# MLP down projection: a third seven-product pair in each quad job, and product banks released by two sums

## The chip, the core and the metric

One core of one Trainium2 chip. The metric is device time in microseconds for one execution of the program. The engines in play: TensorE (PE, matmuls and weight loads), VectorE (DVE), ScalarE (ACT), GpSimd (POOL, a few small operations) and SyncE (SP), which issues the loads of the weights.

## The reference, cut to what matters

Two transformer-like blocks on 256 tokens of width 2048, in float32. The change lies in the MLP of the first one:

```python
u = jax.nn.relu(rms_norm(h, mlp_norm_g) @ w_up)    # 256 x 8192
h = h + (u * u) @ w_down                           # 8192 x 2048
```

Behind it follow an HGRN2 mixer and a convolutional FFN, which the change does not touch.

## The kernel before

Every weight is streamed once, in **windows** of 128 x 1024 float32 (512 KB). SP loads a window into one of six `raw` slots. ACT copies it, rounded, to `w_high` (line 1275), DVE takes `raw - w_high` to `w_low` (line 1594); both have five slots (`AHEAD`), so the split of window s waits until PE is done with window s-5. A product is then three matmuls: high x high, high x low, low x high. Activations are split the same way (`act_high`, `act_low`).

A program (`PLAN`) lists jobs, each a run of windows that adds up in PSUM banks, and puts the other steps at windows. `walk` gives every engine the same order: at window w first the steps put early, then the splits of w+5, then the steps put late. An engine works through its list in order, so a step put between two splits delays all that follow.

The MLP has four blocks of 2048 hidden columns (`FF_BLOCKS`). For each block, four pairs of "features" jobs make the up projection (u, squared, split: `u_square`, `u_split`). The down projection of a block comes next. In blocks 1 to 3 it is two **quad jobs** (c = 0 and c = 2), each for 2 x 512 output columns; block 4 has one quad job and two ordinary token jobs.

A quad job multiplies u (2 tiles of 128 tokens x 16 row chunks) with 16 x 2 blocks of w_down of 128 x 512. Its 16 row chunks are taken in eight pairs (`QUAD_ORDER`). An "eight" pair makes its eight block products in two windows of four products each. A "seven" pair makes the 2x2 by 2x2 block product with seven (Strassen-Winograd forms): two loaded windows and two windows that DVE makes in `raw` from those (`sums_of`, four sums), of which the last is half used. Its windows hold 2, 2, 2 and 1 products. On the activation side it needs sums of blocks of u, the forms (`u_forms`, once a block, for both seven pairs).

Banks: the ordinary sums C of a quad job fill four banks (its own `J` pair, and two of `att`). The products P1, P5, P6 and P7 of the seven pairs gather in the other four, which the job before or behind uses as its C. So PE must wait, at the first window of a job's first seven pair, until the finished banks of the job before have been added to H (`OTHER_EMPTIED`, `add_quads`, line 1930), and at the next job's start until the P banks are read (`add_sevens`). `add_sevens` comes behind the last seven window: ACT copies P1 (line 1482), DVE makes the sums with P6, P7 and P5 and adds them to H (lines 1913 to 1920), eight operations. `h_added` at their end releases the banks.

A job before is 20 windows: eight, seven, eight, eight, seven, eight, eight, eight.

Of the kernel before, what the change touches and what calls it, by code (L numbers as in the profile page):

```python
# [61 lines left out]
QUAD_ORDER = (("eight", 2), ("seven", 0), ("eight", 3), ("eight", 4), ("seven", 1), ("eight", 5), ("eight", 6), ("eight", 7))  # L62
SEVENS = [p for what, p in QUAD_ORDER if what == "seven"]

# [64 lines left out]
class Plan:  # L129
# [71 lines left out]
    "add_sevens": dict(p_copied=1, h_added=1),  # L201
# [142 lines left out]
def plan_mlp(p):  # L344
    for b in range(FF_BLOCKS):
        for j in range(4):
# [4 lines left out]
            p.put(job.end + 1 + 2 * behind, "u_split", j)  # L351
            if j == 0:
                p.put(job.end + 2, "u_forms", b)
# [236 lines left out]
def added():  # L590

    counts, at = Counts(), {}

    def stage(w, name, *args):
        if name in ("add_sevens", "add_quads"):
            at[WINDOW[w][0], name] = counts.at("h_added", 1)
    walk(counts, lambda w: None, lambda w, s: None, stage)
    return at
# [8 lines left out]
def build(nc, d, out):  # L607
    ctx = ExitStack()
    with ctx:
# [12 lines left out]
        forms_both = sb("forms_both", [P, 2, 1024], F32R)  # L622
        H = sb("H", [P, TT, D])
# [70 lines left out]
        form_at = lambda f, p: slice(((f - 1) * 2 + SEVENS.index(p)) * P, ((f - 1) * 2 + SEVENS.index(p) + 1) * P)  # L694
        p1, u_one, u_two = slots[:, 4, 0:COLS], slots[:, 4, COLS:2 * COLS], slots[:, 5, 0:COLS]
# [162 lines left out]
        def _(pe):  # L858
# [30 lines left out]
            def first_of(w):  # L889
# [3 lines left out]
                if k == 0 and job in BEHIND_QUADS:  # L893
                    once("h_added", ADDED[BEHIND_QUADS[job], "add_sevens"])
                if job.kind == "quads" and k == 0 and job in PREVIOUS_QUADS:
                    once("h_added", ADDED[PREVIOUS_QUADS[job], "add_sevens"])
# [48 lines left out]
            def quads(w):  # L945
# [3 lines left out]
                for x, (bank, (of, i, where), cc) in enumerate(job.products(k)):  # L949
# [4 lines left out]
                    else:  # L954
                        once("forms_low", job.needs[1] + 1)
                        ah, al = (a[:, form_at(i, where)] for a in (forms_high, forms_low))
# [290 lines left out]
        def _(act):  # L1247
# [32 lines left out]
            def stage(w, name, *a):  # L1280
# [193 lines left out]
                elif name == "u_forms":  # L1474
                    wait(act, n, "forms_made")
                    wait(act, n, "h_added", 0)
                    nc.scalar.activation(forms_high, forms, ACT.Copy).then_inc(S["forms_high"], 1)
                elif name == "add_sevens":
# [3 lines left out]
                    nc.scalar.activation(p1, quad_bank(buf, ("P", 1)), ACT.Copy).then_inc(S["p_copied"], 1)  # L1482
# [88 lines left out]
        def _(dve):  # L1571
# [59 lines left out]
            def stage(w, name, *a):  # L1631
# [255 lines left out]
                elif name == "u_forms":  # L1887
# [3 lines left out]
                    u = a_slot(2).rearrange("p (q c x t) -> p q c x t", q=2, c=2, x=TT)  # L1891
                    a11, a12, a21, a22 = (u[:, :, c, x, :] for x, c in ((0, 0), (0, 1), (1, 0), (1, 1)))
                    s1, s2, s3, s4 = (forms[:, i * T:(i + 1) * T].rearrange("p (q t) -> p q t", q=2) for i in range(4))
# [6 lines left out]
                    nc.vector.tensor_tensor(forms_low, forms, forms_high.bitcast(F32), ALU.subtract)\  # L1900
# [270 lines left out]
```

## Time and profile before

| | |
|---|---|
| median of 3 runs | 2496.78 us (2496.45 to 2496.8) |
| the profiled execution | 2497.42 us, its span 2495.6 us |
| PE busy | 2476.8 us, 99% of the span |
| DVE busy | 1752.0 us, 70% |
| ACT busy | 1258.2 us, 50% |
| granted TensorE clock, mean | 0.997 |
| weights loaded | 855 windows of 512 KB, median 4.2 us from issue to landing |

Busy time is the time in which an engine has an instruction under way; a matmul's end is modelled, so a busy PE may still be short of its peak, and starts are the safer measure. A row of the timeline gives start and duration, and in brackets the idle time of the engine ahead of it and what ended that. Consecutive instructions of the same kind are merged into one row with their count. The quad jobs lie at 549 to 633, 722 to 807, 896 to 980 and 1069 to 1111 us.

### The profile page before, as it was taken

To read this page: it belongs to the slowest core of one execution; us is meant where nothing else is said; L and a number is where in the kernel's file an instruction comes from. 1 tells how busy PE (TensorE), PEld (TensorE's weight loads), DVE (VectorE), ACT (ScalarE), POOL (GpSimd) and SP (SyncE) were. 2 spreads that over 40 slices of the span, in tenths; PEclk is the share of its full clock that TensorE was granted. 3 is DMA by queue.
4 is the path that set the end of the run, shared out by engine and by line. 5 is a ranking of instruction groups with operands and counts; after the bars stand their busy time and mean duration, and the time that the engine had idled before them with its cause. 6 is when DMAs were issued, how large, how long until landed. Compare 5 with 4: busy or idle time off the path is not lost.

```text
span 2495.6 us, 38061 instructions
## 1 busy us (share of the span) xinstructions
PE 2476.8 (99%) x15416; PEld 2116.1 (85%) x15416; DVE 1752.0 (70%) x1978; ACT 1258.2 (50%) x1506; POOL 29.5 (1%) x26
## 2 busy tenths in 40 slices
PE   9999999999999999999999999999999999999998
PEld 7888888888888888888888888887888888888886
DVE  6656765668668577675777777775777666777777
ACT  7654344545444444445454545454654444444553
POOL 0000000000000000000000000000000000000000
PEclk9999999999999999999999999999999999999999
DMA  9454545546646546565545454555465555556553
GB/s 382 155 189 152 170 157 190 177 162 226 196 169 226 193 171 217 178 211 169 187 154 185 154 185 154 185 185 194 145 216 189 187 193 191 184 190 201 185 188 127
DMA packets 128240, 465.98 MB, mean 187 GB/s; under 512 B 14369, under 2 KB 14625, under 8 KB 127169
## 3 DMA queue, kind: packets, MB, share of 16 engines
q1 hardware_dynamic: 127920, 463.53, 55.1%
q8 instruction: 122, 2.00, 0.3%
q14 instruction: 54, 0.43, 0.1%
q10 hardware_dynamic: 144, 0.02, 0.0%
HBM read 461.39 MB, written 2.10 MB: 186 GB/s over the span
## 4 chain that ended last, share of the span: by engine, by line
PE 96%; issue 3%; DVE 1%; DMA 0%; ACT 0%; SPq 0%; DVEq 0%; POOL 0%; POOLq 0%
PE job L971 31%; PE job L983 16%; PE job L939 11%; PE job L940 11%; PE job L941 11%; PE job L958 2%; PE job L959 2%; PE job L960 2%; PE att L958 2%; PE att L960 2%; PE att L959 2%; PE att L1178 1%; PE att L999 0%; PE att L1011 0%; PE att L1120 0%
## 5 line engine op out<-in xcount | busy, mean ns | idle before, releaser
L1275 ACT ACTIVATE w_high<-raw 128x1024 fp32r<-128x1024 f32 (+1 forms) x883 | 919.8, 1050 | 728.4 <-PE job L941 288.5
L1594 DVE TENSOR_TENSOR w_low<-raw,w_high 128x1024 fp32r<-128x1024 f32 (+1 forms) x883 | 1045.4, 1213 | 303.9 <-ACT w_high L1275 225.9
L971 PE MATMUL job<-actA,w_high 128*128 128x512 f32 x3328 | 799.3, 392 | 0.0
L971 PEld LDWEIGHTS job<-actA,w_high 128*128 128x128 f32 x3328 | 612.8, 189 | 119.5
L983 PEld LDWEIGHTS job<-actA,w_low 128*128 128x128 f32 x3328 | 426.7, 191 | 16.2
L983 PE MATMUL job<-actA,w_low 128*128 128x256 f32 x3328 | 431.7, 283 | 0.0
L1797 DVE TENSOR_TENSOR slots<-job,slots 128x512 f32<-128x512 f32 x102 | 70.5, 691 | 344.0 <-ACT slots L1467 343.3
L939 PE MATMUL job<-w_high,actB 128*128 128x512 f32 x736 | 287.9, 391 | 2.2 <-DVE w_low L1594 1.6
L940 PE MATMUL job<-w_low,actB 128*128 128x512 f32 x736 | 286.5, 389 | 0.0
L941 PE MATMUL job<-w_high,actB 128*128 128x512 f32 x736 | 286.4, 389 | 0.0
L939 PE MATMUL job<-w_high,actA 128*128 128x512 f32 x576 | 230.9, 401 | 0.0
L941 PE MATMUL job<-w_high,actA 128*128 128x512 f32 x576 | 224.5, 390 | 0.0
L940 PE MATMUL job<-w_low,actA 128*128 128x512 f32 x576 | 224.4, 390 | 0.0
L1467 ACT ACTIVATE slots<-job 128x512 f32<-128x512 f32 x102 | 61.0, 598 | 240.6 <-PE job L983 240.6
L939 PEld LDWEIGHTS job<-w_high,actB 128*128 128x128 f32 x736 | 138.2, 188 | 31.8 <-DVE w_low L1594 2.0
L941 PEld LDWEIGHTS job<-w_high,actB 128*128 128x128 f32 x736 | 138.2, 188 | 28.8
L940 PEld LDWEIGHTS job<-w_low,actB 128*128 128x128 f32 x736 | 138.2, 188 | 27.9
L941 PEld LDWEIGHTS job<-w_high,actA 128*128 128x128 f32 x576 | 108.1, 188 | 23.3
L939 PEld LDWEIGHTS job<-w_high,actA 128*128 128x128 f32 x576 | 108.1, 188 | 22.5
L940 PEld LDWEIGHTS job<-w_low,actA 128*128 128x128 f32 x576 | 108.2, 188 | 20.7
L958 PE MATMUL job<-w_high,actB 128*128 128x512 f32 x210 | 81.7, 389 | 0.0
L959 PE MATMUL job<-w_low,actB 128*128 128x512 f32 x210 | 81.7, 389 | 0.0
(257 smaller groups left out, 1906.1 us busy)
## 6 DMA issues: line engine op xcount, KB each, us to landing
raw<-in_weights SPq DMA_DIRECT2D x855, 512.0 KB, 4.2
M<-in_mem_t SPq DMA_DIRECT2D x8, 256.0 KB, 7.9
slots<-in_mem SPq DMA_DIRECT2D x2, 1024.0 KB, 12.2
M<-in_x_t SPq DMA_DIRECT2D x4, 512.0 KB, 13.6
H<-in_x SPq DMA_DIRECT2D x2, 1024.0 KB, 9.0
out<-H SPq DMA_DIRECT2D x8, 256.0 KB, 3.2
slots<-in_w_small SPq DMA_DIRECT2D x1, 1024.0 KB, 10.3
slots<-in_post_mix_g SPq DMA_DIRECT2D x1, 1024.0 KB, 4.8
```

The source lines that it names most:

```text
L939: nc.tensor.matmul(to, ah, w_high[:, slot, cols], start=begins and cc == 0, stop=False)
L940: nc.tensor.matmul(to, ah, w_low[:, slot, cols], start=False, stop=False)
L941: mm = nc.tensor.matmul(to, al, w_high[:, slot, cols], start=False, stop=ends and cc == job.per - 1)
L958: nc.tensor.matmul(to, ah, w_high[:, w % AHEAD, cols], start=(k, x) in job.firsts, stop=False)
L959: nc.tensor.matmul(to, ah, w_low[:, w % AHEAD, cols], start=False, stop=False)
L960: mm = nc.tensor.matmul(to, al, w_high[:, w % AHEAD, cols], start=False, stop=(k, x) in job.lasts)
L971: mm = nc.tensor.matmul(J[job.buf][:, x, :], w_high[:, w % AHEAD, cols], act_both[job.act][:, c, :, :].rearrange("p a t -> p (a t)"), star ...
L983: mm = nc.tensor.matmul(J[job.buf][:, x, T:2 * T], w_low[:, w % AHEAD, cols], act_high[job.act][:, c, :], start=False, stop=ends and cc == ...
L1275: nc.scalar.activation(w_high[:, s % AHEAD, cols], raw[:, s % RAW_SLOTS, cols], ACT.Copy)\
L1467: nc.scalar.activation(by_feature(JOIN[to][:, half_ * COLS:(half_ + 1) * COLS]), J[buf][:, :, T:2 * T], ACT.Copy).then_inc(S["low_copied"], 1)
L1594: nc.vector.tensor_tensor(w_low[:, s % AHEAD, cols], raw[:, s % RAW_SLOTS, cols], w_high[:, s % AHEAD, cols].bitcast(F32), ALU.subtract).t ...
L1797: nc.vector.tensor_tensor(x, J[buf][:, :, 0:T], x, ALU.add).then_inc(S["joined"], 1)
```

## The change

Three pairs of eight are done by seven products, where two were, and they alternate with eights: eight 3, seven 0, eight 4, seven 1, eight 5, seven 2, eight 6, eight 7. A quad job gets 22 windows with 61 products (before 20 with 62). The second seven starts at window 8 (before 10), the third at 14, and four windows (before six) follow the last seven. There are seven quad jobs.

The third pair's forms have a place of their own (`more_forms`, `more_high`, `more_low`) and are made after the second quarter of u (`u_forms` with j = 1). The last quarter's split is moved by two windows. ACT copies P5 too, and the next job waits for the new event `sevens_read`, counted when DVE has made its two sums with P6 and P7, where it waited for `h_added` at the end of all eight operations.

```diff
--- before.py
+++ after.py
@@ -59,9 +59,7 @@
 
 MEM_SET, X_SET, MLP_SET, PREMIX_SET, PREFFN_SET = range(5)
 
-QUAD_ORDER = (("eight", 2), ("seven", 0), ("eight", 3), ("eight", 4), ("seven", 1), ("eight", 5), ("eight", 6), ("eight", 7))
-SEVENS = [p for what, p in QUAD_ORDER if what == "seven"]
-
+QUAD_ORDER = (("eight", 3), ("seven", 0), ("eight", 4), ("seven", 1), ("eight", 5), ("seven", 2), ("eight", 6), ("eight", 7))
 O_EVENT = {2: 1, 3: 2, 0: 3, 1: 4}
 
 
@@ -198,7 +196,7 @@
     "u_square": dict(u_squared=1),
     "u_split": dict(u_high=1, u_low=1),
     "u_forms": dict(forms_made=1, forms_high=1, forms_low=1),
-    "add_sevens": dict(p_copied=1, h_added=1),
+    "add_sevens": dict(p_copied=1, sevens_read=1, h_added=1),
     "add_quads": dict(h_added=1),
     "f_sigmoid": dict(f_sigmoid=1),
     "f_make": dict(f_ready=1),
@@ -348,9 +346,9 @@
                               f"u{j % 2}", False)
             behind = 3 if j == 3 else 0
             p.put(job.end + behind, "u_square", j)
-            p.put(job.end + 1 + 2 * behind, "u_split", j)
-            if j == 0:
-                p.put(job.end + 2, "u_forms", b)
+            p.put(job.end + 1 + 3 * behind - behind // 3, "u_split", j)
+            if j < 2:
+                p.put(job.end + 2, "u_forms", b, j)
         paired = (0, 2) if b < FF_BLOCKS - 1 else (0,)
         for c in paired:
             job = p.quads("B", "w_down", c * COLS, range(b * KC, (b + 1) * KC), ("u_low", b), b * KC)
@@ -593,7 +591,7 @@
 
     def stage(w, name, *args):
         if name in ("add_sevens", "add_quads"):
-            at[WINDOW[w][0], name] = counts.at("h_added", 1)
+            at[WINDOW[w][0], name] = counts.at("sevens_read" if name == "add_sevens" else "h_added", 1)
     walk(counts, lambda w: None, lambda w, s: None, stage)
     return at
 
@@ -620,6 +618,7 @@
         act_both = {n: sb(f"act{n}", [P, KC, 2, T], F32R) for n in "AB"}
         act_high, act_low = ({n: act_both[n][:, :, part, :] for n in "AB"} for part in (0, 1))
         forms_both = sb("forms_both", [P, 2, 1024], F32R)
+        more_both = sb("more_both", [P, 2, COLS], F32R)
         H = sb("H", [P, TT, D])
         M = sb("M", [P, TT, D])
         slots = sb("slots", [P, 10, 1024])
@@ -691,8 +690,16 @@
         post_g = a2(6)
 
         forms, forms_high, forms_low = m_slot(0), forms_both[:, 0, :], forms_both[:, 1, :]
-        form_at = lambda f, p: slice(((f - 1) * 2 + SEVENS.index(p)) * P, ((f - 1) * 2 + SEVENS.index(p) + 1) * P)
-        p1, u_one, u_two = slots[:, 4, 0:COLS], slots[:, 4, COLS:2 * COLS], slots[:, 5, 0:COLS]
+        more_forms = m_slot(1)[:, 0:COLS]
+        more_high, more_low = more_both[:, 0, :], more_both[:, 1, :]
+
+        def form_of(part, f, p):
+
+            if p < 2:
+                at = ((f - 1) * 2 + p) * P
+                return (forms_high, forms_low)[part][:, at:at + P]
+            return (more_high, more_low)[part][:, (f - 1) * P:f * P]
+        p1, u_one, u_two, p5 = (slots[:, 4 + i // 2, i % 2 * COLS:(i % 2 + 1) * COLS] for i in range(4))
         z_conv, y_gate, y_value, y_sig, y = a_slot(0), a_slot(1), a_slot(2), a_slot(3), a_slot(4)
 
         JOIN = {"u0": a_slot(0), "u1": a_slot(1), "f0": hg["f"][0], "f1": hg["f"][1], "q": hg["q"], "z": z_conv,
@@ -891,9 +898,9 @@
                 if k == 0 and job in EMPTIED:
                     once(*EMPTIED[job])
                 if k == 0 and job in BEHIND_QUADS:
-                    once("h_added", ADDED[BEHIND_QUADS[job], "add_sevens"])
+                    once("sevens_read", ADDED[BEHIND_QUADS[job], "add_sevens"])
                 if job.kind == "quads" and k == 0 and job in PREVIOUS_QUADS:
-                    once("h_added", ADDED[PREVIOUS_QUADS[job], "add_sevens"])
+                    once("sevens_read", ADDED[PREVIOUS_QUADS[job], "add_sevens"])
                 if job.kind == "quads" and part_of(w) == 0:
                     once(*OTHER_EMPTIED[job])
                     if job in PREVIOUS_QUADS:
@@ -952,8 +959,8 @@
                         once("u_low", 4 * job.needs[1] + i // 4 + 1)
                         ah, al = (a["B"][:, i, where * P:(where + 1) * P] for a in (act_high, act_low))
                     else:
-                        once("forms_low", job.needs[1] + 1)
-                        ah, al = (a[:, form_at(i, where)] for a in (forms_high, forms_low))
+                        once("forms_low", 2 * job.needs[1] + 1 + where // 2)
+                        ah, al = (form_of(part, i, where) for part in (0, 1))
                     to = quad_bank(job.buf, bank)
                     nc.tensor.matmul(to, ah, w_high[:, w % AHEAD, cols], start=(k, x) in job.firsts, stop=False)
                     nc.tensor.matmul(to, ah, w_low[:, w % AHEAD, cols], start=False, stop=False)
@@ -1474,12 +1481,14 @@
                 elif name == "u_forms":
                     wait(act, n, "forms_made")
                     wait(act, n, "h_added", 0)
-                    nc.scalar.activation(forms_high, forms, ACT.Copy).then_inc(S["forms_high"], 1)
+                    to, of = ((forms_high, forms), (more_high, more_forms))[a[1]]
+                    nc.scalar.activation(to, of, ACT.Copy).then_inc(S["forms_high"], 1)
                 elif name == "add_sevens":
                     buf, c = a
                     act.wait_ge(window_done, w + 1)
                     wait(act, n, "h_added", 0)
-                    nc.scalar.activation(p1, quad_bank(buf, ("P", 1)), ACT.Copy).then_inc(S["p_copied"], 1)
+                    nc.scalar.activation(p1, quad_bank(buf, ("P", 1)), ACT.Copy)
+                    nc.scalar.activation(p5, quad_bank(buf, ("P", 5)), ACT.Copy).then_inc(S["p_copied"], 1)
                 elif name == "f_sigmoid":
                     direction = a[0]
                     f, k = hg["f"][direction], hg["KS"][direction]
@@ -1888,16 +1897,19 @@
 
                     wait(dve, n, "u_squared", 0)
                     wait(dve, n, "forms_high", 0)
-                    u = a_slot(2).rearrange("p (q c x t) -> p q c x t", q=2, c=2, x=TT)
+                    raw_forms, high, low = ((forms, forms_high, forms_low), (more_forms, more_high, more_low))[a[1]]
+                    q = 2 - a[1]
+                    u = a_slot(2 + a[1])[:, 0:q * COLS].rearrange("p (q c x t) -> p q c x t", q=q, c=2, x=TT)
                     a11, a12, a21, a22 = (u[:, :, c, x, :] for x, c in ((0, 0), (0, 1), (1, 0), (1, 1)))
-                    s1, s2, s3, s4 = (forms[:, i * T:(i + 1) * T].rearrange("p (q t) -> p q t", q=2) for i in range(4))
+                    s1, s2, s3, s4 = (raw_forms[:, i * q * P:(i + 1) * q * P].rearrange("p (q t) -> p q t", q=q)
+                                      for i in range(4))
                     done(nc.vector.tensor_tensor(s1, a21, a22, ALU.add))
                     done(nc.vector.tensor_tensor(s2, s1, a11, ALU.subtract))
                     nc.vector.tensor_tensor(s3, a11, a21, ALU.subtract)
                     nc.vector.tensor_tensor(s4, a12, s2, ALU.subtract).then_inc(S["forms_made"], 1)
                     wait(dve, n, "h_added", 0)
                     wait(dve, n, "forms_high")
-                    nc.vector.tensor_tensor(forms_low, forms, forms_high.bitcast(F32), ALU.subtract)\
+                    nc.vector.tensor_tensor(low, raw_forms, high.bitcast(F32), ALU.subtract)\
                         .then_inc(S["forms_low"], 1)
                 elif name == "add_sevens":
 
@@ -1907,17 +1919,17 @@
                     wait(dve, n, "rstd_h", 0)
                     wait(dve, n, "turned", 0)
                     wait(dve, n, "p_copied")
-                    p5, p6, p7 = (quad_bank(buf, ("P", i)) for i in (5, 6, 7))
-                    hh = lambda t, i, k=1: H[:, t, (c + i) * COLS:(c + i + k) * COLS]
+                    p6, p7 = (quad_bank(buf, ("P", i)) for i in (6, 7))
+                    hh = lambda t, i: H[:, t, (c + i) * COLS:(c + i + 1) * COLS]
                     r0, r1 = rstd2[:, 0:1], rstd2[:, 1:2]
                     done(nc.vector.tensor_tensor(u_one, p6, p1, ALU.add))
+                    nc.vector.tensor_tensor(u_two, p7, u_one, ALU.add).then_inc(S["sevens_read"], 1)
                     nc.vector.scalar_tensor_tensor(hh(0, 0), p1, r0, hh(0, 0), ALU.mult, ALU.add)
-                    nc.vector.tensor_tensor(u_two, p7, u_one, ALU.add)
-                    done(nc.vector.tensor_tensor(u_one, p5, u_one, ALU.add))
+                    done(nc.vector.tensor_tensor(u_one, u_one, p5, ALU.add))
                     nc.vector.scalar_tensor_tensor(hh(0, 1), u_one, r0, hh(0, 1), ALU.mult, ALU.add)
                     nc.vector.scalar_tensor_tensor(hh(1, 0), u_two, r1, hh(1, 0), ALU.mult, ALU.add)
-                    done(nc.vector.scalar_tensor_tensor(hh(1, 1), u_two, r1, hh(1, 1), ALU.mult, ALU.add))
-                    nc.vector.scalar_tensor_tensor(hh(1, 1), p5, r1, hh(1, 1), ALU.mult, ALU.add)\
+                    done(nc.vector.tensor_tensor(u_two, u_two, p5, ALU.add))
+                    nc.vector.scalar_tensor_tensor(hh(1, 1), u_two, r1, hh(1, 1), ALU.mult, ALU.add)\
                         .then_inc(S["h_added"], 1)
                 elif name == "add_quads":
```

## Rows read from the trace of the kernel before

**Rows 1.** The page: busy time, and the chain that ended last, by engine.
```profile
PE 2476.8 (99%) x15416; PEld 2116.1 (85%) x15416; DVE 1752.0 (70%) x1978; ACT 1258.2 (50%) x1506; POOL 29.5 (1%) x26
...
PE 96%; issue 3%; DVE 1%; DMA 0%; ACT 0%; SPq 0%; DVEq 0%; POOL 0%; POOLq 0%
```

**Rows 2.** Busy time by stretch: up projection; quad jobs of blocks 1 and 3.
```profile
core 0: us, PE busy (x) PEld busy (x) DVE busy (x) ACT busy (x) POOL busy (x), PEclk, DMA share, GB/s
459.00:548.00 89.00, 89.00 (x514) 78.63 (x514) 53.66 (x57) 42.92 (x50) 0.70 (x1) 1.00 0.51 172
548.00:634.00 86.00, 86.00 (x384) 71.34 (x383) 73.16 (x82) 43.60 (x46) 0.00 (x0) 1.00 0.61 211
888.00:974.00 86.00, 86.00 (x396) 71.81 (x396) 71.15 (x80) 41.85 (x44) 0.00 (x0) 1.00 0.56 199
```

**Rows 3.** PE: its timeline at 548.76, 590.95 and 596.39; its group in 548.5:633.
```profile
548.76 0.40 PE L958 MATMUL job<-w_high,actB 128*128 128x512 f32 x1
...
590.95 0.39 PE L958 MATMUL job<-w_high,actB 128*128 128x512 f32 x1
...
596.39 0.39 PE L958 MATMUL job<-w_high,actB 128*128 128x512 f32 x1
...
L958 PE MATMUL job<-w_high,actB 128*128 128x512 f32 x60 | 23.4, 389 | 0.0
```

**Rows 4.** DVE's timeline, first quad job and the start of the second.
```profile
554.07 5.24 DVE L1594 TENSOR_TENSOR w_low<-raw,w_high 128x1024 fp32r<-128x1024 f32 x5 [1.13 <-ACT w_high L1275]
559.22 1.22 DVE L1879 SCALAR_TENSOR_TENSOR slots<-slots 128x1024 f32<-128x1024 f32 x1
560.35 2.35 DVE L1594 TENSOR_TENSOR w_low<-raw,w_high 128x1024 fp32r<-128x1024 f32 x2
563.41 1.23 DVE L1594 TENSOR_TENSOR w_low<-raw,w_high 128x1024 fp32r<-128x1024 f32 x1 [0.70 <-ACT w_high L1275]
564.55 0.68 DVE L1604 TENSOR_TENSOR raw<-raw 128x512 f32<-128x512 f32 x1
...
568.42 1.23 DVE L1594 TENSOR_TENSOR w_low<-raw,w_high 128x1024 fp32r<-128x1024 f32 x1 [1.13 <-ACT w_high L1275]
...
570.70 6.36 DVE L1594 TENSOR_TENSOR w_low<-raw,w_high 128x1024 fp32r<-128x1024 f32 x6
576.98 0.68 DVE L1913 TENSOR_TENSOR slots<-att,slots 128x512 f32<-128x512 f32 x1
...
582.47 5.76 DVE L1594 TENSOR_TENSOR w_low<-raw,w_high 128x1024 fp32r<-128x1024 f32 x5
588.14 0.68 DVE L1604 TENSOR_TENSOR raw<-raw 128x512 f32<-128x512 f32 x1
...
592.00 1.23 DVE L1594 TENSOR_TENSOR w_low<-raw,w_high 128x1024 fp32r<-128x1024 f32 x1 [1.12 <-ACT w_high L1275]
593.15 1.40 DVE L1930 SCALAR_TENSOR_TENSOR H<-job,rstd,H 128x512 f32<-128x512 f32 x2
594.47 1.40 DVE L1930 SCALAR_TENSOR_TENSOR H<-att,rstd,H 128x512 f32<-128x512 f32 x2
```

**Rows 5.** SP's and ACT's timelines: an issue, two splits behind it, a copy.
```profile
555.32 0.81 SPq L777 DMA_DIRECT2D raw<-in_weights  x2
...
558.63 1.06 ACT L1275 ACTIVATE w_high<-raw 128x1024 fp32r<-128x1024 f32 x1 [1.23 <-DMA raw<-in_weights]
560.11 1.07 ACT L1275 ACTIVATE w_high<-raw 128x1024 fp32r<-128x1024 f32 x1 [0.41 <-DMA raw<-in_weights]
...
575.18 0.58 ACT L1482 ACTIVATE slots<-job 128x512 f32<-128x512 f32 x1
```

**Rows 6.** DVE's groups in the MLP: the split of the forms.
```profile
L1900 DVE TENSOR_TENSOR forms_both<-M,forms_both 128x1024 fp32r<-128x1024 f32 x4 | 4.9, 1225 | 4.8 <-ACT forms_both L1477 4.8
```

**Rows 7.** PE's timeline around its longest wait, and busy time in 1752:1754.
```profile
1744.32 0.39 PE L941 MATMUL job<-w_high,actB 128*128 128x512 f32 x1
1748.49 3.65 PE L999 MATMUL att<-ident,H 128*128 128x128 f32 x16 [3.79 <-DVE H L1986]
1751.79 3.34 PE L971 MATMUL job<-actA,w_high 128*128 128x512 f32 x8
...
1752.00:1754.00 2.00, 2.00 (x6) 1.59 (x6) 2.00 (x6) 1.17 (x4) 0.00 (x0) 0.50 0.00 0
```

## The prediction

> **What bounds the kernel now.** The page's busy time and its chain come first: the matrix engine (PE) is busy for 2476.8 of 2495.6 us, and the chain that ended last runs through PE for 96% [rows 1]. So fewer matmuls pay only where PE really is what is late. The busy time by stretch comes next. In the two quad jobs of the first MLP block (548 to 634 us) PE is busy for all 86 us, but VectorE (DVE) already for 73.2, against 53.7 of 89 in the up projection before them; the third block's pair of quad jobs looks the same, 71.2 [rows 2]. The reader is to see two engines near their limit here, and to ask which one the change loads. Then PE's rows: the first quad job's first matmul starts at 548.76, the next job's at 590.95, 186 matmuls later, so 0.2268 us from one to the next, and its lines show no idle time before them [rows 3]. The DVE rows of the same job are what decides [rows 4]: apart from a few waits for ScalarE (ACT) there is no hole in them from 554 to 597 us.
>
> I count windows of a job from w0, those of the next job as w0'. A block product is 3 matmuls, 0.68 us. A window of an eight pair is 12 matmuls, 2.72 us. The four windows of a seven pair are 6, 6, 6 and 3 matmuls, 4.76 us together.
>
> **What the change takes from PE.** One product in each of seven quad jobs: 7 x 3 x 0.2268 = 4.76 us. If nothing else moved, that would be 0.19% of the time.
>
> **What it adds to DVE.** From DVE's rows [rows 4]: a low split of 1024 columns costs 1.14 (582.47 to 588.14 holds five), and the half one of a fourth window 0.60 (570.70 to 576.98 holds five whole ones and one half). The sums of a seven pair run from 564.55, and the low split behind them starts at 568.42: 3.87, of which 1.13 is DVE waiting while ACT makes the high part of the sums. An eight pair costs DVE 2 x 1.14 = 2.28 for 5.44 us of PE. A seven pair costs 3 x 1.14 + 0.60 + 3.87 = 7.89 for 4.76 us of PE. So each exchange adds 5.6 us to DVE and takes 0.7 us from PE. DVE's whole load of a first quad job then exceeds PE's 41.5 us. That is the argument; the rest is where it becomes late.
>
> **First quad job of a block, window by window.** Up to w8 the order on DVE is as before: low splits of w3 to w7 from 554.07, the square of the last quarter at 559.22, w8 at 560.35 [rows 4]. Before, two further splits of eight pairs followed, and the sums of the second seven came with w11; now they come with w9, straight behind w8, at 561.49. The raw block that they need was there at 560.11 [rows 5].
> - w9: low split starts 561.49 + 3.87 = 565.36, ends 566.6 (1.23 long). With 0.2 for a weight load PE can start at 566.8. It would want to at 548.76 + 75 x 0.2268 = 565.77. Stall 1.05.
> - From 565.36: w9 1.14, w10 1.14, w11 0.60, w12 1.14, w13 1.14, the moved low split of u 1.14, w14 1.14 gives 572.8; sums and wait 3.87; the low split of w15 starts at 576.7 and ends at 577.9. PE wants w15 at 566.8 + 45 x 0.2268 = 577.0 and gets it at 578.1. Stall 1.1.
> - w15 to w19 bring DVE to 581.8. The raw blocks of w20 and w21 are asked for only when the low split of w15 is done. Before, two such loads were issued at 555.32, and ACT could start on the blocks at 558.63 and 560.11 [rows 5], 3.3 and 4.8 us later; here 581.2 and 582.7, plus 1.06 of ACT each. So w20 and w21 start at 582.3 and 583.8 on DVE, 0.9 later than by DVE alone, and DVE comes to the sevens' sums at 585.0.
> - These are eight operations of 5.49 us before (576.98 to 582.47) [rows 4], and eight of the same sizes after. That they read a copy of P5 in place of the bank changes no length that I can see; the second copy costs ACT 0.58 [rows 5], which lies beside DVE's queue (counted in the 585.0). They end at 590.5.
> - w0', w1', w2' 3 x 1.14 = 593.9; sums and wait, 597.8; w3', 598.9; then the four additions of the finished banks, 2.7 us from 593.15 to 595.87 before [rows 4], now 598.9 to 601.6.
>
> **The wait that matters is the last one.** At w2', the first window of the next job's first seven pair, PE waits until those four additions are done, since P1, P5, P6 and P7 take over the banks that they empty. Before, they ended at 595.87 and w2' started at 596.39 [rows 3, 4], a margin of 0.3 after the weight load. Now PE is at w2' at 548.76 + 183 x 0.2268 + 2.15 + 5.44 = 597.85 and gets going at 601.85: stall 4.0. Against 596.39 before, w2' is 5.45 late. Behind PE in this wait stand all matmuls; behind those, ACT's and DVE's splits, which need the five split buffers back.
>
> **Second quad job.** The stall gives DVE its lead back. From 601.6: w4' to w8' to 606.7, sums, the low split of w9' ends at 611.8, where PE wants it at 601.85 + 51 x 0.2268 = 613.4. The sums of w15' wait for a load that is asked for at 611.8, and the split ends at 622.5; PE wants it at 623.6. So no stall here, with leads of 1.6 and 1.1, and the job saves its 0.68. The up projection that follows has room: DVE busy 53.7 of 89 [rows 2].
>
> **Release by two sums.** The next job may start when DVE has read P6 and P7, 4 us ahead of the end of its eight operations. In the working above that is 586.5 instead of 590.5, and PE starts that job at 592.4: it was hidden and stays hidden. Worth nothing, except that with the old release the cover would be down to 1.9.
>
> **Forms.** The third seven's forms (four sums of 128 columns, a copy and a split of 512) come once a block in the up projection. The twice as large ones there take DVE 4.9 / 4 = 1.2 for the split and 1.2 of waiting each [rows 6], with no PE wait; so between 0 and nothing visible, I take 0. The later square and split of u's last quarter are read first at w18; they are done at 571.7.
>
> **Sum.** Blocks 1 to 3 (two quad jobs each): 5.45 - 0.68 = 4.8 each, 14.3. Block 4 (one quad job, then ordinary token jobs): 1.05 + 1.1 - 0.68 = 1.5; there the additions end at 597.7 on the same scale and the transposes that need them come at 597.8, so 0 to 0.5 more. Together +16.0. The profiled span 2495.6 becomes 2511.6, and the median 2496.78 (1.2 above the span) becomes 2512.8, +0.64%.
>
> **The clock.** A 4 us stall is just the size that cost the clock once already. At 1744.32 PE's last matmul before a wait starts; it idles 3.79 us, the next work starts at 1748.49, and the granted clock is 0.50 from 1752 to 1754, the lower level of 1.2 GHz [rows 7]. There 8 matmuls of 512 columns took 3.34 us, 0.42 each, in place of 0.2268. If that happens at w2', some 6 us of matmuls at the lower level, 15 of them, cost 15 x 0.19 = 2.9 us each time, 8.7 for three. The Trainium skill, in "TensorE: Matmul & The Clock Gate", part 1, says that the throttled state is the default and activity releases it; by that rule the change would pay twice for a stall. The row agrees for one wait of 3.79; at 4.0 I can't tell from it whether each of three falls, since the one row is at the edge of what I forecast.
>
> **Rivals.**
> 1. *Forecast*: DVE becomes the bound in the quad jobs, w2' waits, the clock holds. 2512.8. Chance 0.50.
> 2. *The clock falls* at some or all of the three waits at w2': 2515.7 (one) to 2521.5 (three). For it: the 3.79 us row. Against it: my wait could be 1 us shorter. 0.27.
> 3. *Second jobs stall too*: their leads of 1.6 and 1.1 rest on loads that land in 3.3 and 4.8 us; 2 us more each gives 1.3 more a job or so, and the same in first jobs: about +6, 2519. 0.08.
> 4. *Only the early waits count*: DVE runs about 4 us faster than I add up (a wait of it that overlaps), so the additions are in time at w2'. Then 4 x 2.15 - 4.76 = +3.8, 2500.6, within 0.2%. 0.10.
> 5. *The other side, faster*: DVE's room. Over both jobs DVE is busy 73.2 of 86 us [rows 2], so 12.8 are free, and two exchanges want 2 x 4.5 of busy time (5.6 less the wait of 1.13). If five split buffers and six raw ones smooth this over both jobs, nothing stalls and the whole 4.76 comes out: 2492.0. It decides from the point where DVE's lag at a job's end stays under the lead that it has at w2'. Against it: that lead is 0.3 now, and DVE's free time lies in the second job, behind w2'. 0.05.
>
> About 0.2%, 5 us, is what a measurement of this kernel tells from no change. Slower 0.85, same 0.10, faster 0.05. The range leaves out rivals 4 and 5 and reaches to three falls of the clock: 2503 to 2523.
>
> **What would show it.** PE in the quad jobs: waits of about 1 us at w9 and w15 of each first job, released by DVE's low splits (line 1594), and one of about 4 us at w2' released by DVE's additions to H (line 1930 before), three times. DVE without holes from 550 to 602. Second quad jobs without PE waits. The granted clock in the stretch after w2'. The prediction is wrong if PE has no waits there, or if the splits at w9 come earlier than 1.1 us behind PE: then the length that I gave to sums and wait (3.87) is not what a seven pair costs.

## The result: 1% slower, by waits and by the clock behind them

The changed kernel takes 2522.48 us (median of 4 runs, 2520.42 to 2523.47), the kernel before 2496.67 beside it: ratio 1.0102, 95% interval 1.0089 to 1.0114. Forecast was 2512.8 in a range of 2503 to 2523, and 2521.5 for the rival in which the clock falls three times.

The page of the changed kernel, against [rows 1], shows 21 matmuls fewer and 35 us more of DVE work. Of the chain that ended last, 8 points have gone from PE to DVE, ACT, the loads and issue.

```profile
PE 2483.8 (98%) x15395; PEld 2116.6 (84%) x15395; DVE 1787.3 (71%) x2040; ACT 1272.1 (50%) x1531; POOL 28.6 (1%) x26
...
PE 88%; issue 5%; DVE 4%; ACT 1%; DMA 1%; DVEq 0%; SPq 0%; POOL 0%; ACTq 0%; POOLq 0%
```

Busy time by stretch, the quad jobs of blocks 1 and 3 (columns as in [rows 2]). The pairs last about 7.5 us longer. PE, which was busy throughout, has 6.4 and 5.1 us of holes in 94, DVE is at 80 of 94, and the granted clock is below 1:

```profile
core 0: us, PE busy (x) PEld busy (x) DVE busy (x) ACT busy (x) POOL busy (x), PEclk, DMA share, GB/s
550.00:644.00 94.00, 87.55 (x380) 71.17 (x379) 80.19 (x92) 46.78 (x52) 0.00 (x0) 0.98 0.52 185
912.00:1006.00 94.00, 88.92 (x383) 72.52 (x382) 80.46 (x92) 47.40 (x52) 0.00 (x0) 0.96 0.51 185
```

PE's waits in the changed kernel (who for whom: total, times, longest), of which the kernel before has none:

```profile
PE job L965 <- DVE H L1942: 10.9, 3, 4.1
PE att L965 <- DVE w_low L1603: 5.9, 8, 0.8
...
PE job L965 <- DVE w_low L1603: 0.8, 1, 0.8
```

PE's timeline has them at the places named ahead: w9, w15, and w2' of blocks 1, 2 and 3. One more, at 595.42, was not forecast: it stands at w0', the first matmul of block 1's second job. The number in brackets is PE's idle time; a stall reckoned from starts, as in the prediction (start to start, less one matmul of 0.2268), comes out 0.16 us longer.

```profile
568.70 0.50 PE L965 MATMUL att<-w_high,forms_both 128*128 128x512 f32 x1 [0.68 <-DVE w_low L1603]
...
579.99 0.50 PE L965 MATMUL att<-w_high,more_both 128*128 128x512 f32 x1 [0.79 <-DVE w_low L1603]
...
595.42 0.47 PE L965 MATMUL job<-w_high,actB 128*128 128x512 f32 x1 [0.85 <-DVE w_low L1603]
...
605.23 0.50 PE L965 MATMUL job<-w_high,actB 128*128 128x512 f32 x1 [4.13 <-DVE H L1942]
...
784.48 0.80 PE L965 MATMUL job<-w_high,actB 128*128 128x512 f32 x1 [3.20 <-DVE H L1942]
...
965.58 0.79 PE L965 MATMUL job<-w_high,actB 128*128 128x512 f32 x1 [3.61 <-DVE H L1942]
```

DVE's timeline of the first job, against [rows 4], shows four things. Each chain of sums and split is as long as before (563.55 to 567.42 is 3.87). There is no hole between the chains. One wait of 2.30 stands at the split of w20: ACT had no block to copy there, because it waited for the load. And the four additions come behind the next job's sums:

```profile
562.42 1.22 DVE L1603 TENSOR_TENSOR w_low<-raw,w_high 128x1024 fp32r<-128x1024 f32 x1
563.55 0.68 DVE L1613 TENSOR_TENSOR raw<-raw 128x512 f32<-128x512 f32 x1
...
567.42 5.23 DVE L1603 TENSOR_TENSOR w_low<-raw,w_high 128x1024 fp32r<-128x1024 f32 x5 [1.13 <-ACT w_high L1282]
...
578.71 5.23 DVE L1603 TENSOR_TENSOR w_low<-raw,w_high 128x1024 fp32r<-128x1024 f32 x5 [1.13 <-ACT w_high L1282]
586.24 2.47 DVE L1603 TENSOR_TENSOR w_low<-raw,w_high 128x1024 fp32r<-128x1024 f32 x2 [2.30 <-ACT w_high L1282]
588.63 0.68 DVE L1925 TENSOR_TENSOR slots<-att,slots 128x512 f32<-128x512 f32 x1
...
601.32 1.23 DVE L1603 TENSOR_TENSOR w_low<-raw,w_high 128x1024 fp32r<-128x1024 f32 x1 [1.12 <-ACT w_high L1282]
602.46 1.41 DVE L1942 SCALAR_TENSOR_TENSOR H<-job,rstd,H 128x512 f32<-128x512 f32 x2
603.78 1.40 DVE L1942 SCALAR_TENSOR_TENSOR H<-att,rstd,H 128x512 f32<-128x512 f32 x2
```

Behind each of the three long waits the granted clock is 0.50, the lower of its two levels, 1.2 GHz:

```profile
606.00:609.00 3.00, 3.00 (x8) 2.32 (x7) 2.31 (x4) 1.06 (x1) 0.00 (x0) 0.50 0.15 59
784.50:790.00 5.50, 5.50 (x13) 4.35 (x14) 4.02 (x4) 1.06 (x1) 0.00 (x0) 0.50 0.49 182
966.00:970.00 4.00, 4.00 (x10) 3.04 (x10) 2.70 (x4) 1.06 (x1) 0.00 (x0) 0.50 0.32 115
```

**Where the 26.05 us of span went**, from starts of matmuls. w2' comes 54.40, 52.41 and 52.78 us after the first job's start in blocks 1, 2 and 3, where it came after 47.63: +6.8, +4.8, +5.15, together 16.7. From w2' to the start of the pair's last product 37.12, 38.60 and 38.11, where 35.36 are due (36.04 before, less the product saved): the low clock costs 1.8, 3.2 and 2.75, together 7.75. Three products saved there, -2.0. Block 4, first to last product, +1.4. That is 23.8. A further 2.07 lies ahead of the MLP: the first quad job starts at 550.83, where it was 548.76, and in the runs below, most of which have all that the change has up to there, it starts between 548.1 and 549.7. It is not the change's. It was there after the first 17 us of the program: the 51st matmul starts at 16.84, before at 14.78, and the granted clock is low for the matmuls from 12.10 to 15.40, behind a wait that ended at 11.93. The kernel before waits 1.55 there and stays at the full clock. The rest, 0.2, is behind the MLP.

```profile
11.93 0.70 PE L946 MATMUL job<-w_high,actB 128*128 128x512 f32 x1 [1.96 <-DVE w_low L1603]
...
12.10:15.40 3.30, 3.30 (x8) 2.57 (x9) 3.12 (x6) 2.96 (x6) 0.00 (x0) 0.50 1.03 415
```

### The profile page after: what moved, and what is told of

It reads as the page before. It is cut to its first block, busy times and chain, and to the rows that moved or that the text cites. A ratio compares the mean times of both kernels' runs of the same rounds, so it can differ in the third digit from the quotient of the medians.

```text
span 2521.7 us, 38157 instructions
## 1 busy us (share of the span) xinstructions
PE 2483.8 (98%) x15395; PEld 2116.6 (84%) x15395; DVE 1787.3 (71%) x2040; ACT 1272.1 (50%) x1531; POOL 28.6 (1%) x26
## 4 chain that ended last, share of the span: by engine, by line
PE 88%; issue 5%; DVE 4%; ACT 1%; DMA 1%; DVEq 0%; SPq 0%; POOL 0%; ACTq 0%; POOLq 0%
PE job L978 30%; PE job L990 16%; PE job L946 11%; PE job L947 11%; PE job L948 11%; DVE w_low L1603 2%; PE job L965 1%; PE job L967 1%; PE job L966 1%; ACT w_high L1282 1%; PE att L965 1%; PE att L966 1%; PE att L967 1%; DMA raw<-in_weights 1%; PE att L1185 1%
## 5 line engine op out<-in xcount | busy, mean ns | idle before, releaser
L1603 DVE TENSOR_TENSOR w_low<-raw,w_high 128x1024 fp32r<-128x1024 f32 (+1 forms) x897 | 1056.9, 1208 | 306.3 <-ACT w_high L1282 231.5
L946 PE MATMUL job<-w_high,actB 128*128 128x512 f32 x736 | 288.6, 392 | 3.2 <-DVE w_low L1603 2.0
L947 PE MATMUL job<-w_low,actB 128*128 128x512 f32 x736 | 287.3, 390 | 0.0
L948 PE MATMUL job<-w_high,actB 128*128 128x512 f32 x736 | 286.9, 390 | 0.0
L965 PE MATMUL job<-w_high,actB 128*128 128x512 f32 x203 | 80.8, 398 | 11.8 <-DVE H L1942 10.9
L967 PE MATMUL job<-w_high,actB 128*128 128x512 f32 x203 | 80.2, 395 | 0.0
```

Source lines behind the costliest of these rows:

```text
L946: nc.tensor.matmul(to, ah, w_high[:, slot, cols], start=begins and cc == 0, stop=False)
L947: nc.tensor.matmul(to, ah, w_low[:, slot, cols], start=False, stop=False)
L948: mm = nc.tensor.matmul(to, al, w_high[:, slot, cols], start=False, stop=ends and cc == job.per - 1)
L965: nc.tensor.matmul(to, ah, w_high[:, w % AHEAD, cols], start=(k, x) in job.firsts, stop=False)
L967: mm = nc.tensor.matmul(to, al, w_high[:, w % AHEAD, cols], start=False, stop=(k, x) in job.lasts)
L1603: nc.vector.tensor_tensor(w_low[:, s % AHEAD, cols], raw[:, s % RAW_SLOTS, cols], w_high[:, s % AHEAD, cols].bitcast(F32), ALU.subtract).t ...
```

## Experiments

The theory after the result: a third seven gives DVE 5.6 us more work per job, more than it can hide in the first job of a pair. DVE's lag becomes PE's wait at the banks of w2', and the clock falls for the wait. Rivals: the new order by itself; the release or the copy of P5; the loads; low clock from another cause. Each kernel is the changed one with an edit, of which the lines that matter are shown; each has runs of the kernel before beside it. In `two_by_turns_b` and `release_only` the forms of a third seven are left out too, and in `release_only`, `second_only` and `second_early` the split of u's last quarter is back in its old place.

### Order or third seven?

```diff
-QUAD_ORDER = (("eight", 3), ("seven", 0), ("eight", 4), ("seven", 1), ("eight", 5), ("seven", 2), ("eight", 6), ("eight", 7))
+QUAD_ORDER = (("eight", 2), ("seven", 0), ("eight", 3), ("seven", 1), ("eight", 4), ("eight", 5), ("eight", 6), ("eight", 7))
```

> The changed kernel with two sevens again, but by turns: eight 2, seven 0, eight 3, seven 1, eight 4 to eight 7; the second seven starts at window 8 as in the change, the release and the copy of P5 are kept. It parts the new order from the third seven. Theory (the third seven's DVE work is the cause): only the wait ahead of the second seven remains, 0.85 in each of the four first jobs and none at window 2: 2500.2. Rival (sevens too close to each other are the cause): most of the loss of 26 us is here too.

It takes 2501.08, ratio 1.0016 (1.0007 to 1.0026). There is one wait of 0.68 idle in each of the four first jobs and none at w2':

```profile
PE att L965 <- DVE w_low L1603: 2.7, 4, 0.7
```

So the order by itself costs 4 us, because no second eight stands between the first two sevens. The rest comes with the third seven.

> The order and the count of sevens of the kernel before, with the change's release by two sums and its copy of P5 by ACT. Every theory: no difference, 2496.7 within 0.5 us, as the release comes some 8 us ahead of its use in either form. If the second copy in ACT's queue or the other order of DVE's eight operations cost something, it would show here.

```diff
-QUAD_ORDER = (("eight", 3), ("seven", 0), ("eight", 4), ("seven", 1), ("eight", 5), ("seven", 2), ("eight", 6), ("eight", 7))
+QUAD_ORDER = (("eight", 2), ("seven", 0), ("eight", 3), ("eight", 4), ("seven", 1), ("eight", 5), ("eight", 6), ("eight", 7))
```

It takes 2497.62 against 2497.67 before, ratio 0.9999 (0.9990 to 1.0008). The release and the copy of P5 have no part in the loss.

### Is it DVE's queue?

```diff
                     nc.vector.tensor_tensor(u_two, p7, u_one, ALU.add).then_inc(S["sevens_read"], 1)
-                    nc.vector.scalar_tensor_tensor(hh(0, 0), p1, r0, hh(0, 0), ALU.mult, ALU.add)
                     done(nc.vector.tensor_tensor(u_one, u_one, p5, ALU.add))
-                    nc.vector.scalar_tensor_tensor(hh(0, 1), u_one, r0, hh(0, 1), ALU.mult, ALU.add)
-                    nc.vector.scalar_tensor_tensor(hh(1, 0), u_two, r1, hh(1, 0), ALU.mult, ALU.add)
```

> The changed kernel without three of the eight DVE operations on the seven pairs' sums (three of the four additions to H behind u_one and u_two), so part of the MLP's output is left out. 2.0 us less DVE work in each quad job, nothing else. Theory (DVE's queue is what is late, one for one): the wait at window 2 of the second jobs shrinks by 2.0 to about 2 us idle each, the clock holds, the early waits of 0.85 and 0.95 stay: 3 x 2.0 + 7.2 less than the changed kernel, 2509. Rival (PE waits for something else, the loads or ACT): under 2 us of change.

2511.93 (2509.96 to 2517.19), ratio 1.0062. w2' starts 52.60, 50.90 and 50.93 us into the pair: 1.8, 1.5 and 1.85 earlier for 2.0 us of DVE work less. The waits are 3.41, 1.72 and 1.73 idle; the clock falls behind the first and holds at the others. That is 3 us more than expected, and the trace shows two reasons, both of them loads. In block 1 the wait stayed long: DVE waited 2.44 ahead of `add_sevens` for a split whose load was late, against 0.8 in all in each of the other blocks. And block 2's second job now waits 1.14 at its third seven, behind a wait of DVE of 2.45 that a load ended. In block 3, where the wait at w2' was equally short, DVE waited 0.38 at that place and PE not at all.

```diff
             p.put_early(job.end, "add_quads", job.buf, c)
+            if c == 0 and len(paired) == 2:
+                p.splits[job.end - 1], p.splits[job.end] = [], (job.end + 4, job.end + 5)
```

> The changed kernel with the order on DVE and ACT turned round at one place: the additions of the first quad job's finished banks come ahead of the sums and the split of the next job's window 3, not behind them. Theory: the additions end at about 600 in place of 605 us, so the wait at window 2 is gone; but the split of window 3 comes at 605.2 where PE wants it at 602.3, so a wait of 3.1 start to start (2.7 idle) takes its place. If the clock holds at 2.7 idle: 3 x 1.1 + 7.2 less than the changed kernel, 2512. If it falls all the same: 2519. Rival (the wait at window 2 is the only trouble, DVE's total is not): all of its 4 us and the clock go, 2505 or less.

2515.73, ratio 1.0074. The bank wait is gone and the split of w3' is late instead, in block 1 after 3.13 start to start, where 3.1 was expected:

```profile
602.35 0.57 PE L967 MATMUL att<-w_high,forms_both 128*128 128x512 f32 x1 [2.74 <-DVE w_low L1605]
```

In blocks 2 and 3 it is 2.25 and 2.49 idle and the clock holds; in block 1 it falls, and again behind a wait of 2.02 at the third seven of block 2's second job. (DVE waited 2.28 for a load there too.) Hence 2515.7 between my 2512 and 2519. The wait at w2' was where DVE's lag showed, not its cause.

### The clock

> The changed kernel with nine more matmuls in each second quad job: window 1 ends with nine products of a zero block that are added to its own banks, 2.0 us of matmuls that change no sum. They lie in PE's order right ahead of the wait at window 2 (idle 4.1, 3.2 and 3.6 us in the changed kernel) and shorten the idle time, not the wait's end. Theory (the late DVE makes the wait, and the wait makes the clock fall): idle there about 2 us, no low clock behind it, and 7.2 us less than the changed kernel (the matmuls at the lower level are gone: 1.4 + 3.0 + 2.8), 2515.3, between 2513 and 2517.5. Rival (the low clock stretches have another cause, or cost nothing because DVE is late anyway): 2522 as before.

```diff
+                if k == 1 and job in BEHIND_QUADS:
+                    pe.wait_ge(zero_made, 1)
+                    for i in range(FILL):
+                        mm = nc.tensor.matmul(quad_bank(job.buf, ("C", 1, i % 2))[0:32, :], zero[:, :],
+                                              w_high[:, w % AHEAD, 0:COLS], start=False, stop=False)
```

It takes 2520.9, ratio 1.0094, where 2515.3 was expected. The idle time did shrink to 2.0, but the clock was low behind all three waits:

```profile
604.31 0.50 PE L968 MATMUL job<-w_high,actB 128*128 128x512 f32 x1 [2.02 <-DVE H L1952]
...
605.20:608.00 2.80, 2.80 (x8) 2.21 (x7) 2.15 (x4) 1.06 (x1) 0.00 (x0) 0.50 0.13 54
```

It left open whether 2.0 us idle are enough, or zeros on 32 columns are not work like the rest. So, with twelve real products:

> The changed kernel with twelve real matmuls more at the end of window 1 of each second quad job: the last product's operands once more, added to that job's own banks, so the MLP's output has terms too many. 2.7 us of matmuls ahead of the wait at window 2, with full weights in place of the zero block of 32 columns. Theory (a long enough idle stretch of PE makes the clock fall; the runs so far had no fall at idle times up to 1.73 us, three falls and three holds between 2.0 and 2.5 without the zero block, and a fall at each of 2.7 or more): idle about 1.3 us, no low clock, 5.1 us less than the run with the zero block (2520.9), so 2516. Rival (what went before in the job, not the idle stretch, lowers the clock): low stretches at the same three places, 2521.

```diff
+                if k == 1 and job in BEHIND_QUADS:
+                    for i in range(FILL):
+                        mm = nc.tensor.matmul(quad_bank(job.buf, ("C", 1, i % 2)), ah, w_high[:, w % AHEAD, cols],
+                                              start=False, stop=False)
```

```profile
597.74 2.88 PE L971 MATMUL att<-w_high,actB 128*128 128x512 f32 x12
602.01 0.50 PE L966 MATMUL job<-w_high,actB 128*128 128x512 f32 x1 [1.39 <-DVE H L1947]
...
602.00:608.00 6.00, 5.99 (x26) 4.99 (x27) 5.83 (x6) 2.13 (x2) 0.00 (x0) 1.00 0.54 189
```

It takes 2514.01 (2513.49 to 2514.47), ratio 1.0067. There is no low clock in the MLP, although PE waits for the same additions, 1.39, 1.39 and 0.99 idle. From w2' to the last product each block needs 35.50, near the 35.36 that are due; over the three blocks that is 7.3 us less than in the changed kernel, with 36 matmuls more. That the two times are 8.5 apart, near the 7.75 that the clock cost, is partly chance: of the 9.0 between the profiled spans, 2.4 lie ahead of the first quad job, and w2' comes 1.3 later in all. What is shown is that with a shorter idle stretch at the same places the clock does not fall. Which share the zeros' kind had in the other run is not shown. The expectation says that the clock had fallen at each idle time of 2.7 or more; in one of the runs that it counts, `later_old_release` (below), it had held behind 2.73.

### The loads

```diff
-                    sp.wait_ge(low_ready, w - RAW_SLOTS + 1 + (part_of(w - RAW_SLOTS) == 0))
+                    sp.wait_ge(low_ready, w - RAW_SLOTS + 1)
+                    if part_of(w - RAW_SLOTS) == 0:
+                        sp.wait_ge(sums_made, SUMS[w - RAW_SLOTS + 1])
```

> The changed kernel with one wait of SP's loads changed: the load that takes over the raw slot of a seven pair's first window waits for that window's own split and for the sums, no longer for the split of the window behind it; it can start 2.4 us earlier. The order of all engines is the same. Theory (part of the wait at window 2 is DVE waiting for the load of window 20: 2.30, 0.33 and 0.69 us in the three pairs of the changed kernel's trace, 2.4, 2.1 and 1.8 in the run with the zero block): these go, and the second jobs' window 2 starts 52.1 us after the first job in each pair, where it was 54.4, 52.4 and 52.8; the wait itself stays about 3 us idle and the clock still falls. 2522.5 - 3.3 or a little more: 2518 to 2519.5. Rival (DVE's queue alone sets it, the load's wait only fills time it has): no change.

It takes 2513.98, ratio 1.0070. DVE's waits ahead of `add_sevens` are 1.14, 0 and 0 in place of 2.30, 0.33 and 0.69, and w2' starts 53.16, 51.91 and 51.92 into the pair (52.1 expected).

```profile
584.30 1.23 DVE L1605 TENSOR_TENSOR w_low<-raw,w_high 128x1024 fp32r<-128x1024 f32 x1 [1.14 <-ACT w_high L1284]
...
780.70 0.50 PE L967 MATMUL job<-w_high,actB 128*128 128x512 f32 x1 [2.70 <-DVE H L1944]
```

That is 2.6 us in all. The other 5 to 6 are the clock, which held at 2.70 and 2.73 idle where I had expected it to fall. The wait of block 1, 3.97, and its fall remain.

### Another place for the three sevens

```diff
-QUAD_ORDER = (("eight", 3), ("seven", 0), ("eight", 4), ("seven", 1), ("eight", 5), ("seven", 2), ("eight", 6), ("eight", 7))
+QUAD_ORDER = (("eight", 3), ("eight", 4), ("seven", 0), ("eight", 5), ("seven", 1), ("eight", 6), ("seven", 2), ("eight", 7))
```

> The changed kernel, all three sevens, but each two windows later: eight 3, eight 4, seven 0, eight 5, seven 1, eight 6, seven 2, eight 7. The wait for the earlier job's banks is then at window 4, 5.4 us of matmuls later, and on DVE the additions come ahead of the next sums. Theory (DVE is nearly full but not over; what cost was where its lag meets the bank wait): in the first jobs DVE's splits lead by 2.2 us at the second seven and by 1.1 at the third; in the second jobs one wait of about 0.8 at the first seven; the next job starts without a wait, since P6 and P7 are read at 587.8 where PE comes at 590.3. -4.8 + 3 x 0.8: 2494.3, between 2492 and 2498. Rival (a third seven is more than DVE can do in a quad job, wherever it stands): 2505 or more.

It takes 2509.51, ratio 1.0044 (1.0032 to 1.0057): half the loss is gone, but it is 15 over what I expected. The wait at w5' is 2.3 to 2.4 idle, not 0.8, as DVE waited some 1.8 us in the first job, in part for loads, and the clock fell behind two of three. And in block 4 the transposes wait for additions that are late there, which my working of this order had left out:

```profile
604.35 0.58 PE L965 MATMUL att<-w_high,forms_both 128*128 128x512 f32 x1 [2.32 <-DVE w_low L1603]
...
1126.72 0.54 PE L1006 MATMUL att<-ident,H 128*128 128x128 f32 x2 [3.34 <-DVE H L1942]
```

The same with `once("h_added", ...)` in place of `once("sevens_read", ...)`, that is the release of the kernel before:

> The kernel of the run with each seven two windows later, with the old release: PE waits at the next job's start until all eight operations behind the sevens are done, not only the two sums with P6 and P7. Theory (there the release is worth something, since only two windows lie behind the last seven): waits of about 1.6 us at the start behind each first job and up to 2.6 behind each second job, 4 x 1.6 + 3 x 2.6 at most: 2502 to 2508. Rival (the release is hidden here too): as the run without this edit, 2494.

It takes 2529.39 (2523.89 to 2531.87), ratio 1.0118, where 2502 to 2508 was expected. It is 20 us over the run above, by waits of 2.7 to 3.8 at the next job's start, behind DVE's eighth operation, and low clock behind six of these seven. So the release by two sums is worth much where two windows lie behind the last seven, and nothing where six do (`release_only`). For the four windows of the change only the trace speaks: there the eight operations end at 594.13, 773.38 and 954.47, and the next jobs start at 595.42, 775.68 and 956.37.

```profile
594.11 0.50 PE L965 MATMUL job<-w_high,actB 128*128 128x512 f32 x1 [3.71 <-DVE H L1932]
```

> Three sevens in the six paired quad jobs, each seven two windows later than in the change; the single quad job of block 4 keeps the two sevens of the kernel before; with the earlier load. Against the run with later sevens alone: block 4 loses its 3.3 us wait of the transposes for the additions, and the waits for loads (0.59, 0.5, 0.41 and 0.32 us on DVE in the first pair) go, so the split of window 5 of the second jobs comes 1.8 earlier and the wait there is 0.5 to 0.9 us in place of 2.3, too short for the clock to fall. 6 x 0.68 less 3 x 0.8: 1.7 below the kernel before, between 3 below and 1 above. Rival (DVE's total is over PE's in a first job, so no order helps): 4 or more above.

Its edit is the later order, the earlier load, and for block 4 the order of the kernel before, with two sevens. It takes 2498.03 against 2497.04, ratio 1.0003 (0.9994 to 1.0012); 1.7 below was expected. There are waits of 1.36 to 1.41 idle at w5', no low clock, and no wait in block 4. That is eleven us better than with the later order alone, and no gain: each pair saves 1.36 and loses 1.7, 1.5 to 1.6 of it in that wait. Which of the two further edits gave how much was not run.

### The third seven where there is room

```diff
-            job = p.quads("B", "w_down", c * COLS, range(b * KC, (b + 1) * KC), ("u_low", b), b * KC)
+            job = p.quads("B", "w_down", c * COLS, range(b * KC, (b + 1) * KC), ("u_low", b), b * KC,
+                          QUAD_ORDER if c else TWO_ORDER)
```

(`TWO_ORDER` is the order of the kernel before, the constructor takes the order as an argument.)

> The changed kernel with the third seven only in the second quad jobs of blocks 1 to 3; the first jobs have the order of the kernel before, with two. Theory (the second jobs have DVE time to spare, as the changed kernel's trace shows no PE wait over 0.1 us in them): no waits at all, and three products saved, 3 x 0.68 = 2.0: 2494.7. Rival (the second jobs were only free because the 4 us wait ahead of them let DVE catch up): waits of about 1 us at the second or third seven, 2497 or more.

It takes 2496.42 against 2497.67, ratio 0.9995 (0.9986 to 1.0004), not to be told from no change. One wait of 0.56 is left, in block 3, behind a DVE wait of 1.89 for a load. With the earlier load:

> The third seven only in the second quad jobs of blocks 1 to 3, with the earlier load of the slot of a seven pair's first window. Without the earlier load one PE wait of 0.56 was left in the third block. Theory: that wait goes, no PE wait is left in the quad jobs, and all of 3 x 0.68 = 2.0 us is gained: 2.0 below the kernel before, ratio 0.9992. If the load had no part in that wait: 1.2 below.

It takes 2494.73 against 2497.04, ratio 0.9990 (0.9981 to 0.9999): 2.3 us faster than the kernel before, barely clear of its interval, where 2.0 was expected, and 28 faster than the change. PE has no hole in any of the three pairs; the first:

```profile
548.00:632.00 84.00, 84.00 (x375) 69.63 (x374) 75.30 (x86) 45.30 (x49) 0.00 (x0) 1.00 0.61 205
```

Why there is room in the second job can be read in the kernel before, whose first pair is cut here at the second job's start:

```profile
core 0: us, PE busy (x) PEld busy (x) DVE busy (x) ACT busy (x) POOL busy (x), PEclk, DMA share, GB/s
548.76:590.95 42.19, 42.19 (x188) 34.92 (x187) 38.01 (x43) 21.54 (x24) 0.00 (x0) 1.00 0.55 199
590.95:633.10 42.15, 42.15 (x187) 34.91 (x186) 34.46 (x37) 21.43 (x22) 0.00 (x0) 1.00 0.66 223
```

DVE has 4.2 us without work during the first job and 7.7 during the second, and a third seven takes 5.6 of its queue.

## Why the prediction was right, and where it was off

- **DVE becomes the bound, first at w9 and w15.** Right. Stalls of 1.05 and 1.1 forecast, 0.84 and 0.95 measured (start to start, less one matmul).
- **The wait at w2'.** Right in place, releaser and size: a stall of 4.0 forecast, 4.29, 3.36 and 3.77 measured (idle 4.13, 3.20 and 3.61). w2' late by 5.45 forecast, by 6.8, 4.8 and 5.15 measured. The term that was mis-sized is the one for the loads of w20 and w21: 0.9 forecast; 2.30, 0.33 and 0.69 measured. In block 1 that also gave the wait of 0.85 at w0', which I did not have; it lies inside the lateness of w2'.
- **Second jobs without waits.** Behind w2' right in the changed kernel, 0.08 at most. The leads of 1.1 and 1.6 rest on the loads, as rival 3 says: `fewer_adds_b` showed a wait of 1.14 and `adds_first_b` one of 2.02 at such a third seven, each behind a load that DVE waited for.
- **Sum without the clock**: +16.0 forecast; 16.7 - 2.0 + 1.4 = 16.1 measured. That it fits so well is partly luck: the load term was 1.4 too small in one block and 0.6 and 0.2 too large in the others.
- **The clock** is the step that failed. I gave the case that it holds 0.50 and made it the forecast, and its falls 0.27. They came at all three waits and cost 7.75 (8.7 in the rival). The one row [rows 7] had 3.79 us idle and a fall, and nothing in the trace showed a wait of that length without one; calling it the edge had no row behind it. The rule of the Trainium skill ("TensorE: Matmul & The Clock Gate", part 1, that the throttled state is the default) spoke for the rival, and the traces agree with it: eleven of eleven waits of 3.2 us or more were followed by the low clock.
- **The range** holds the result by 0.5 us, at its upper end, which was put at three falls of the clock. That the time comes so near to the 2521.5 of that rival is also chance: 2.07 us of the profiled run lie ahead of the MLP and belong to no term of the sum.
- **Release** worth nothing here: right by `release_only` for six windows and by the trace for the four of the change. The cover left with the old release, 1.9 forecast, was 2.3 and 1.9 in blocks 2 and 3; in block 1 the late load had used it up but for 0.3, by starts. It holds for a long tail of eights alone.
- **The other side** (DVE's room of 12.8 us in a pair): the room is there, but most of it in the second job. `second_early` takes it there and gains; no order tried here gained it in the first job.

## What to carry to other kernels

Ask of the helper engine's queue not its share of busy time but its lag at each point where the main engine waits for it. Here a fifth of a per cent of matmul work was exchanged for work on a queue with 15% free, and the loss was five times what it should have saved, because most of that free time lay in the second half of the stretch and the third seven's lag came due at its middle. Price a forecast wait of the matmul engine of more than about 2 us with the low clock behind it: in these runs the clock fell behind 19 of 25 waits of 2.0 us or more. And put the cheaper algorithm only into those jobs whose helper has room.

## What the hardware showed that was not expected

The clock does not follow the idle time alone. In the quad jobs of all runs, and where the next job waits for them, there was no low clock behind idle times up to 1.73 us, eight times in fourteen behind 2.0 to 2.8 us (low at 2.02, held at 2.49 and 2.73), and every time, eleven of eleven, behind 3.2 us or more. Three of the eight are those behind the zero products. In the first 17 us of the changed kernel it fell behind 1.96, and at the same place of `filled_wait_b` it held behind 2.28. How much work it slowed varied as well: in the changed kernel seven matmuls at 0.43 us apart in block 1, and twelve or thirteen in blocks 2 and 3, so that a fall cost 1.8 to 3.2 us. In block 1 the granted clock was still 1.00 for the first 0.7 us behind the wait; in blocks 2 and 3 it was at 0.50 about 1 us before the wait ended.

A load asked for at the same place in three equal blocks made DVE wait 2.30, 0.33 and 0.69 us in the changed kernel and 2.4, 2.1 and 1.8 in the one with zero products, whose first jobs have the same instructions. What varied it was not found.
